# Latent attention by head: values stationary in two column halves, probabilities normalised before they are turned, gates produced turned, and changed places for sums and stops

## The chip, the cores and the metric

One core of one Trainium2 chip runs the whole program. The metric is the time of one execution in microseconds of device time (us). Below, TensorE, VectorE, ScalarE, GpSimd and SyncE are the core's engines; SyncE issues the loads of the weights.

## The reference, cut to what matters

Two blocks of two layers each work on x of 256 rows (tokens) and 1024 columns, all in float32. The first block mixes three attention branches. The second block has an even layer (windowed attention with a sink and a gated MLP, for x and for a context of 256 rows) and an odd layer with latent attention; the final norm follows.

```python
# even layer, for the 256 rows of x and the 256 rows of the context
q, k, v, u, vv, gate = split(h @ w_in0)
a = sink_attention(rope(q), rope(k), v)          # 8 heads of 64
b = gelu(u) * (w_s @ layer_norm(gelu(vv)) + b_s)
y = (concat(a, b) * silu(gate)) @ w_out0
# odd layer: latent attention, queries of x only, keys and values of x and context
q_a, kv_a, k_pe, gate = split(h @ w_in1)         # 256, 128, 32, 1024
q = rms_norm(q_a) @ w_qb                          # 16 heads of 64 + 32
k, v = rms_norm(kv_a) @ w_kvb                     # 16 heads, v of 64
p = softmax(q @ k.T * 96 ** -0.5)                 # 256 x 512 for each head
y = (concat_heads(p @ v) * silu(gate)) @ w_out1
# in every layer: shift, scale, gate = silu(c) @ w_ada + b_ada  (w_ada is 1024 x 3072)
```

## The kernel before, in words

Every engine's program is written out by hand, in order; nothing is rescheduled. Matmul results go to eight PSUM banks. A table of units (`units_of_layer_e`, `units_of_layer_o`) numbers every use of a bank, and `begin`, `done`, `filled`, `emptied` and `free` turn it into waits on two semaphores for each bank.

**The ring.** All weights are cut into chunks of up to 2 MB (`CH1`, `CHE`, `CHO`) that pass through three slots, in that order. SyncE has one program: it waits until the last user of chunk c-3 is done, and then issues the load of chunk c (L577). So a load also stands behind the waits of all loads before it. In the even layer the chunks are e_kv, e_q, e_u, e_vv, e_g0, adag4, e_ws, e_g1, adag5, ada0, ada1, e_o0, e_o1, ada2, ada3, and then those of the odd layer, o_kv, o_q, adah4, o_g0 and so on. An ada chunk is summed over its 1024 rows on TensorE in four column groups of 32 (`ada_rows`, L656), copied out by ScalarE, and brought to columns (`ada_columns`, L664).

**The start.** Four ada chunks are summed while x is normalised and turned; then the first projection, idx, waits for hT, which ScalarE and VectorE scale out of PSUM.

**Even layer.** `E_ORDER` is (2, 3, 0, 1): the context's row blocks first. The projections e_q, e_u and e_vv (`E_SPLIT`) are made of three fast products of high and low parts: ScalarE rounds rows to xhi and pieces of weights to whi, VectorE takes the differences xlo and wlo, TensorE multiplies (L1061). Then follow 15 steps g. In each TensorE does what the tables `E_GATES` (a gate projection of 8 matmuls of 512 columns, L1026), `E_SUMS` (`ada_rows`) and `E_ADA` (`ada_columns`) set for it, then turns two units of probabilities (L688, step 2 on), makes the logits of two units (L1115) and multiplies two turned units with the values (L1095, step 3 on). Step 4 has the gated MLP (L1146), steps 12 and 13 broadcast the gates gb (L1039). The output projection follows, with the remaining sums in `E_OUT_SUMS` and `E_OUT_ADA`.

**Odd layer.** o_kv, o_q, the gates o_g0 and o_g1 (rows on partitions), keys okT, values ova, queries oqT. The SiLU of all 2 x 1024 gate columns is one ScalarE operation (L1676). Then 16 steps of latent attention, two units (a block of 128 queries and a head) in each, by block first (`O_UNITS`). TensorE: logits of step p (L1243, 512 columns each), four transposes for each unit of step p-1 (L688), and four value matmuls for each unit of step p-2, with turned probabilities stationary and 64 columns of values moving (L1259). VectorE: maximum of each unit (L2478), its scaling (L2480), the copy of every second turned unit (L2484). ScalarE: exponentials (L1538) and the other copies (L1299). Per 8 heads `o_gated` scales by the reciprocal of the sums and multiplies with the gate (L2460, L2465). The result is turned with 16 transposes, copied to hT2, and projected.

## Time and profile before

| what | before |
|---|---|
| three runs, us | 1175.83, 1175.37, 1170.96; median 1175.37 |
| the profiled execution, us | 1175.9 (span 1174.1) |
| TensorE busy | 1118.2 us, 95% of the span |
| TensorE weight loads, beside it | 702.6 us, 60% |
| VectorE, ScalarE, GpSimd busy | 518.6 (44%), 410.6 (35%), 95.8 (8%) |
| chain that ended last | TensorE 82%, VectorE 8%, ScalarE 6%, DMA 3% |
| mean granted clock of TensorE | 0.988 |

The profiled execution is one run of the program; its span runs from the first instruction to the last, and its own time is 1.8 us longer. The chain is followed back from the last instruction, at each step to what released it. The even layer's steps stand at 771 to 895 us, its output projection at 896 to 964, the odd layer behind it, the latent attention at 1061 to 1137.

### The profile page before, as it was taken

To read this page: it belongs to the slowest core of one execution; us is meant where nothing else is said; L and a number is where in the kernel's file an instruction comes from. 1 tells how busy PE (TensorE), PEld (TensorE's weight loads), DVE (VectorE), ACT (ScalarE), POOL (GpSimd) and SP (SyncE) were. 2 spreads that over 40 slices of the span, in tenths; PEclk is the share of its full clock that TensorE was granted. 3 is DMA by queue.
4 is the path that set the end of the run, shared out by engine and by line. 5 is a ranking of instruction groups with operands and counts; after the bars stand their busy time and mean duration, and the time that the engine had idled before them with its cause. 6 is when DMAs were issued, how large, how long until landed. Compare 5 with 4: busy or idle time off the path is not lost.

```text
span 1174.1 us, 12609 instructions
## 1 busy us (share of the span) xinstructions
PE 1118.2 (95%) x4876; PEld 702.6 (60%) x4876; DVE 518.6 (44%) x1087; ACT 410.6 (35%) x858; POOL 95.8 (8%) x115
## 2 busy tenths in 40 slices
PE   5999999999999999999999989989999989999997
PEld 2687775644447878655444468845666437345773
DVE  2439765552425488542224342244424133235642
ACT  2436545320025355633300342253534032325431
POOL 3005110000000131100000003100000000230000
PEclk9899999999999999999999999999999998998999
DMA  9644333567334343245574251200415116241000
GB/s 376 232 181 172 149 144 115 214 245 286 143 113 173 157 183 144 104 151 213 210 286 179 78 212 72 90 1 9 208 63 224 72 30 253 80 157 76 1 1 36
DMA packets 13739, 171.23 MB, mean 146 GB/s; under 512 B 1504, under 2 KB 1760, under 8 KB 3056
## 3 DMA queue, kind: packets, MB, share of 16 engines
q1 hardware_dynamic: 12944, 167.77, 37.3%
q10 hardware_dynamic: 736, 2.65, 0.6%
q8 instruction: 39, 0.64, 0.2%
q14 instruction: 20, 0.16, 0.0%
HBM read 169.37 MB, written 1.05 MB: 145 GB/s over the span
## 4 chain that ended last, share of the span: by engine, by line
PE 82%; DVE 8%; ACT 6%; DMA 3%; issue 1%; ACTq 0%; DVEq 0%
PE bank L696 17%; PE bank L1026 16%; PE bank L718 11%; PE bank L990 7%; PE bank L1061 6%; PE bank L688 4%; PE bank L1243 3%; PE bank L1259 2%; PE bank L794 2%; DVE wlo L1986 2%; DMA ring<-in_weights 2%; PE bank L664 2%; PE bank L656 2%; DMA X<-in_x 1%; PE bank L1095 1%
## 5 line engine op out<-in xcount | busy, mean ns | idle before, releaser
L696 PE MATMUL bank<-ring,hT 128*128 128x512 f32 (+1 forms) x576 | 246.3, 584 | 3.2 <-ACT hT L1319 2.4
L1026 PE MATMUL bank<-ring,hT 128*128 128x512 f32 (+2 forms) x544 | 202.2, 530 | 10.1 <-DMA ring<-in_weights 6.3
L696 PEld LDWEIGHTS bank<-ring,hT 128*128 128x128 f32 x576 | 108.9, 193 | 123.3 <-issue 118.5
L1026 PEld LDWEIGHTS bank<-ring,hT 128*128 128x128 f32 x544 | 101.2, 196 | 102.3 <-issue 95.6
L1986 DVE TENSOR_TENSOR wlo<-ring,whi 128x512 fp32r<-128x512 f32 x120 | 89.0, 767 | 40.6 <-ACT whi L1375 40.4
L718 PE MATMUL bank<-whi,xhi 128*128 128x512 f32 (+1 forms) x256 | 99.1, 387 | 6.6 <-DVE wlo L1986 4.7
L718 PE MATMUL bank<-whi,xlo 128*128 128x512 f32 (+1 forms) x256 | 96.5, 377 | 0.0
L718 PE MATMUL bank<-wlo,xhi 128*128 128x512 f32 (+1 forms) x256 | 96.4, 377 | 0.0
L1375 ACT ACTIVATE whi<-ring 128x512 fp32r<-128x512 f32 x120 | 72.7, 630 | 64.3 <-PE bank L718 64.3
L718 PEld LDWEIGHTS bank<-whi,xhi 128*128 128x128 f32 x256 | 48.1, 188 | 21.5 <-issue 7.7
L1299 ACT ACTIVATE G<-bank 128x512 f32<-128x512 f32 x24 | 14.3, 596 | 119.7 <-PE bank L696 119.7
L990 PE MATMUL bank<-ring,X 128*128 128x512 f32 x128 | 55.9, 595 | 0.0
L718 PEld LDWEIGHTS bank<-whi,xlo 128*128 128x128 f32 x256 | 48.2, 188 | 9.1
L718 PEld LDWEIGHTS bank<-wlo,xhi 128*128 128x128 f32 x256 | 48.2, 188 | 7.9
L656 PE MATMUL bank<-ring,cst 128*32 128x512 f32 x224 | 31.5, 686 | 13.5 <-DMA ring<-in_weights 13.5
L1887 DVE SCALAR_TENSOR_TENSOR retqkv<-ring,cst,retqkv 128x512 f32<-128x512 f32 x56 | 42.1, 752 | 2.0
L990 PEld LDWEIGHTS bank<-ring,X 128*128 128x128 f32 x128 | 24.0, 190 | 28.7 <-issue 28.7
L1061 PE MATMUL bank<-whi,xhi 128*128 128x512 f32 x96 | 38.0, 396 | 2.7 <-issue 2.7
L1061 PE MATMUL bank<-wlo,xhi 128*128 128x512 f32 x96 | 38.4, 400 | 0.0
L1061 PE MATMUL bank<-whi,xlo 128*128 128x512 f32 x96 | 37.4, 389 | 0.0
L1299 ACT ACTIVATE LP<-bank 128x512 f32<-128x512 f32 x40 | 22.5, 595 | 39.3 <-PE bank L688 39.3
L2293 DVE TENSOR_TENSOR wlo<-ring,whi 128x1024 fp32r<-128x1024 f32 x12 | 15.4, 1292 | 44.5 <-ACT whi L1552 44.5
(380 smaller groups left out, 1558.5 us busy)
## 6 DMA issues: line engine op xcount, KB each, us to landing
ring<-in_weights SPq DMA_DIRECT2D x73, 2048.0 KB, 8.5
ring<-in_weights SPq DMA_DIRECT2D x5, 1024.0 KB, 5.1
ring<-in_weights SPq DMA_DIRECT2D x2, 1360.0 KB, 7.6
ring<-in_weights SPq DMA_DIRECT2D x1, 1536.0 KB, 9.5
kk<-in_k SPq DMA_DIRECT2D x1, 1120.0 KB, 8.0
X<-in_x ACTq DMA_DIRECT2D x1, 1024.0 KB, 15.8
kc<-in_k ACTq DMA_DIRECT2D x1, 1024.0 KB, 11.7
X<-in_context SPq DMA_DIRECT2D x1, 1024.0 KB, 10.7
```

The costliest lines, as they stand in the source:

```text
L656: mm = pe.matmul(ps[GROUP * g:GROUP * (g + 1), :], cst[:, k, :], ring[:, slot, k * 512:(k + 1) * 512], start=(k < 4), stop=(k >= 4))
L688: mm = pe.transpose(ps[0:n, i * P:(i + 1) * P], blk, ident[:])
L696: mm = pe.matmul(ps[:, 0:width], hT[:, k, t * P:(t + 1) * P], ring[:, slot, k * stride + w0:k * stride + w0 + width], start=(k == 0), stop ...
L718: mm = pe.matmul(o[:, 0:width], a, b[:, q % BUFFERS, at], start=(k == 0 and m == 0), stop=(k == KD - 1 and m == 2))
L990: mm = pe.matmul(ps[:, :], branchT[b][:, k, t * P:(t + 1) * P], ring[:, slot, k * D + h * 512:k * D + h * 512 + 512], start=(k == 0), stop ...
L1026: mm = pe.matmul(ps[:, 0:width], hT2[:, k, t * P:(t + 1) * P], ring[:, slot, k * width:(k + 1) * width], start=(k == 0), stop=(k == KD - 1))
L1061: mm = pe.matmul(o[:, :], a, b[:, q % 2, at], start=(k == 0 and n == 0), stop=(k == KD - 1 and n == 2))
L1243: done(u, f"ml{i}", pe.matmul(ps[:, :], oqT[:, h, t * P:(t + 1) * P], okT[:, h, :], start=True, stop=True))
L1299: act.activation(dst, shape_like(ps[0:dst.shape[0], 0:n], dst), func, scale=scale).then_inc(free(u, name), 1)
L1375: act.activation(whi1[:, q % BUFFERS, :], w, ACT.Copy).then_inc(event("hi1_ready"), 1)
L1887: ins = dve.scalar_tensor_tensor(rows, w, cst[:, k, v:v + 1], rows, ALU.mult, ALU.add)
L1986: dve.tensor_tensor(wlo1[:, q % BUFFERS, :], piece1(q)[2], whi1[:, q % BUFFERS, :], ALU.subtract).then_inc(event("lo1_ready"), 1)
```

## The change

- The latent attention goes by head: the two units of a step are the two query blocks of one head. VectorE normalises the probabilities (`o_normal`: reciprocal of the sum, scaling of 128x512 in place) before they are turned; it makes them in its step p+1, behind the maxima of that step. ScalarE copies all turned units to a new tile PT3. TensorE turns units two steps after their logits, ahead of the step's own logits, and every second step multiplies two heads (`o_values`): values stationary (64 columns), 256 query columns moving, one head in the lower and one in the upper half of the output partitions. The result is already turned: `o_gated` multiplies it with turned gates into hT2, and the 16 transposes and their copies are gone.
- The gates are produced turned (`gates_turned`): weights stationary, 256 row columns moving, 32 matmuls of 256 columns for each half in place of 16 of 512. SiLU of the first half is one ScalarE operation, that of the second half is done while its banks are copied. The scale of the logits moves to the copies of oqT, and the scaling of each maximum is gone.
- Chunk ada2 goes ahead of e_o0 and e_o1; the tables of the even layer's steps change: the second gate projection goes to step 1, adag4 is summed in step 2, adag5 in step 6 (was 9), ada0 in 9 (was 12), ada1 in 12 (was in the output projection).
- In the even layer the split products take row blocks in `E_ORDER`, wait for each block of xlo by itself, and ScalarE and VectorE round rows and weights in a new order.
- Nine matmuls of ones stand before the first projection of layer 0.
- The scratch size for DMA descriptors is 1024.

```diff
--- before.py
+++ after.py
        ("e_g0", KD * 512), ("adag4", KD * 512), ("e_ws", KD * P), ("e_g1", KD * 512), ("adag5", KD * 512),
-       ("ada0", KD * 512), ("ada1", KD * 512), ("e_o0", KD * 512), ("e_o1", KD * 512), ("ada2", KD * 512),
+       ("ada0", KD * 512), ("ada1", KD * 512), ("ada2", KD * 512), ("e_o0", KD * 512), ("e_o1", KD * 512),
        ("ada3", KD * 512)]
...
+BUSY_START = 9
...
-E_GATES = {0: 0, 2: 1, 3: 2, 5: 3, 7: 4, 8: 5, 10: 6, 11: 7}
-E_SUMS = {1: "adag4", 9: "adag5", 12: "ada0"}
-E_ADA = {2: "adag4", 10: "adag5", 13: "ada0"}
+E_GATES = {0: 0, 1: 1, 3: 2, 5: 3, 7: 4, 8: 5, 10: 6, 11: 7}
+E_SUMS = {2: "adag4", 6: "adag5", 9: "ada0", 12: "ada1"}
+E_ADA = {4: "adag4", 7: "adag5", 10: "ada0", 13: "ada1"}
 E_ROWS_AT = {12: 0, 13: 1}
-E_OUT_SUMS = {(0, 0): "ada1", (1, 0): "ada2", (1, 2): "ada3"}
-E_OUT_ADA = {(0, 2): "ada1", (1, 1): "ada2", (1, 3): "ada3"}
+E_OUT_SUMS = {(0, 1): "ada2", (1, 1): "ada3"}
+E_OUT_ADA = {(0, 3): "ada2", (1, 2): "ada3"}
...
-O_UNITS = [(t, h) for t in range(TT) for h in range(MLA_HEADS)]
+O_UNITS = [(t, h) for h in range(MLA_HEADS) for t in range(TT)]
...
-        og = sbo("og", [P, TT, D])
+        og = sbo("og", [P, KD, S])
+        PT3 = sbo("pt3", [P, 4, NT, TT, P])
...
+            def keep_busy(ps, n):
+
+                for i in range(n):
+                    pe.matmul(ps[:, 0:P], ones[:], ones[:], start=True, stop=True)
...
+                if l == 0:
+                    keep_busy(begin(u, "idx0"), BUSY_START)
...
-            pe.wait_ge(event("xlo_ready"), NT)
             for q in range(len(E_SPLIT) * SPLIT_PIECES):
                 name, i = E_SPLIT[q // SPLIT_PIECES], q % SPLIT_PIECES
                 pe.wait_ge(event("lo_ready"), q + 1)
-                for t in range(NT):
+                for n, t in enumerate(E_ORDER):
+                    if q == 0:
+                        pe.wait_ge(event("xlo_ready"), n + 1)
...
-            slot = landed2("o_g0")
-            for t in range(TT):
-                project2(u, f"o_g0{t}", slot, t, 512)
+            def gates_turned(n):
+
+                slot = landed2(f"o_g{n}")
+                for j in range(2):
+                    ps = begin(u, f"o_g{n}{j}")
+                    for a in range(2):
+                        for k in range(KD):
+                            at = k * 512 + (2 * j + a) * P
+                            mm = pe.matmul(ps[:, a * S:(a + 1) * S], ring[:, slot, at:at + P], hT2[:, k, 0:S],
+                                           start=(k == 0), stop=(k == KD - 1))
+                    done(u, f"o_g{n}{j}", mm)
+
+            gates_turned(0)
...
+            def o_turn(i):
+
+                pe.wait_ge(event("o_norm"), i + 1)
+                ps = begin(u, f"mp{i}")
+                done(u, f"mp{i}", turn_blocks(ps, [L2[:, i % 4, b * P:(b + 1) * P] for b in range(4)]))
+
+            def o_values(j):
+
+                for i in range(4 * j, 4 * j + 4):
+                    emptied(pe, u, f"mp{i}")
+                ps = begin(u, f"mo{j}")
+                for b in range(NT):
+                    for r in range(2):
+                        h = 2 * j + r
+                        mm = pe.matmul(ps[64 * r:64 * r + 64, 0:S].rearrange("p (t c) -> p t c", t=TT),
+                                       ova[:, b, h * 64:(h + 1) * 64], PT3[:, h % 4, b], start=(b == 0), stop=(b == NT - 1))
+                done(u, f"mo{j}", mm)
+
+            for p in range(MLA_HEADS + 3):
+                if 2 <= p < MLA_HEADS + 2:
+                    o_turn(2 * p - 4)
+                    o_turn(2 * p - 3)
...
-                if 1 <= p < 17:
-                    for i in (2 * p - 2, 2 * p - 1):
-                        emptied(pe, u, f"ml{i}")
-                        ps = begin(u, f"mp{i}")
-                        done(u, f"mp{i}", turn_blocks(ps, [L2[:, i % 4, b * P:(b + 1) * P] for b in range(4)]))
-                if p >= 2:
-                    for i in (2 * p - 4, 2 * p - 3):
-                        t, h = O_UNITS[i]
-                        emptied(pe, u, f"mp{i}")
-                        if i % 8 == 0:
-                            begin(u, f"mo{i // 8}")
-                        o = bank[u.at[f"mo{i // 8}"][0]]
-                        for b in range(NT):
-                            mm = pe.matmul(o[:, (h % 8) * 64:(h % 8) * 64 + 64], PT2[:, i % 4, b * P:(b + 1) * P],
-                                           ova[:, b, h * 64:(h + 1) * 64], start=(b == 0), stop=(b == NT - 1))
-                        if i % 8 == 7:
-                            done(u, f"mo{i // 8}", mm)
-            for t in range(TT):
-                pe.wait_ge(event("om_ready"), t + 1)
-                for h in range(2):
-                    ps = begin(u, f"oyT{t}{h}")
-                    done(u, f"oyT{t}{h}", turn_blocks(ps, [og[:, t, (4 * h + i) * P:(4 * h + i + 1) * P] for i in range(4)]))
+                if p >= 4 and p % 2 == 0:
+                    o_values(p // 2 - 2)
+            for j in range(MLA_HEADS // 2):
+                emptied(pe, u, f"mo{j}")
             slots = [landed2("o_o0"), landed2("o_o1")]
...
+            def rows_high(t):
+                emptied(act, u, f"xT{t}0")
+                emptied(act, u, f"xT{t}1")
+                act.activation(xhi[:, :, t * P:(t + 1) * P], hT2[:, :, t * P:(t + 1) * P], ACT.Copy).then_inc(event("xhi_ready"), 1)
+
             scale_x2(u, 0, E_ORDER[2])
             norm_x2(0, E_ORDER, E_PARTS, 1, "x_ready", X_E)
+            rows_high(E_ORDER[0])
+            rows_high(E_ORDER[1])
             scale_x2(u, 0, E_ORDER[3])
 
...
             split_high(0)
+            rows_high(E_ORDER[2])
+            rows_high(E_ORDER[3])
             split_high(1)
...
-            act.activation(og[:], og[:], ACT.Silu).then_inc(event("osilu"), 1)
+            act.activation(og[:, 0:4, :], og[:, 0:4, :], ACT.Silu).then_inc(event("osilu"), 1)
+            for j in range(2):
+                copy_out(u, f"o_g1{j}", og[:, 4 + 2 * j:6 + 2 * j, :], func=ACT.Silu)
...
+                copy_rows(u, f"oqT{j}", oqT[:, 2 * j:2 * j + 2, :], ps[0:MLA_QK, :].rearrange("p (a b) -> p a b", a=2),
+                          ACT.Copy, scale=MLA_SCALE)
+            for p in range(MLA_HEADS + 2):
+                if p >= 2:
+                    for i in (2 * p - 4, 2 * p - 3):
+                        t, h = O_UNITS[i]
+                        copy_out(u, f"mp{i}", PT3[:, h % 4, :, t])
...
+            rows_low(0)
+            rows_low(1)
+            split_low(0)
+            rows_low(2)
+            rows_low(3)
+            for q in range(1, len(E_SPLIT) * SPLIT_PIECES):
+                split_low(q)
...
+            def o_gated(j):
+
+                dve.wait_ge(event("osilu"), 1)
+                for i in range(2):
+                    emptied(dve, u, f"o_g1{i}")
+                ps = filled(dve, u, f"mo{j}")
+                dve.tensor_tensor(hT2[:, j, 0:S], ps[:, 0:S], og[:, j, :], ALU.mult).then_inc(free(u, f"mo{j}"), 1)
+
+            def o_normal(i):
+
+                t, h = O_UNITS[i]
+                emptied(dve, u, f"ml{i}")
+                step(dve.reciprocal(r2[:, t, h:h + 1], sm2[:, t, h:h + 1]))
                 settle()
+                dve.tensor_scalar(L2[:, i % 4, :], L2[:, i % 4, :], r2[:, t, h:h + 1], None, ALU.mult).then_inc(event("o_norm"), 1)
+
+            for p in range(MLA_HEADS + 4):
+                if p < MLA_HEADS:
+                        dve.tensor_reduce(mx2[:, t, h:h + 1], ps[:, :], AX, ALU.max, negate=True).then_inc(event("o_max"), 1)
+                if 1 <= p < MLA_HEADS + 1:
+                    o_normal(2 * p - 2)
+                    o_normal(2 * p - 1)
+                if p >= 5 and p % 2:
+                    o_gated((p - 5) // 2)
+    nc = _bacc.Bacc("TRN2", target_bir_lowering=False, num_devices=1, dynamic_dma_scratch_size=1024)
```

TensorE in the even layer, from the gate projection of step 5 to that of step 7. Before:

```order
L1026 MATMUL bank<-ring,hT 128x512 x8
L688 MATMUL bank<-ident,LP 128x128 x8
L1115 MATMUL bank<-ekT,eqT 128x512 x2
L1095 MATMUL bank<-ev,LP 128x64 x8
L688 MATMUL bank<-ident,LP 128x128 x8
L1115 MATMUL bank<-ekT,eqT 128x512 x2
L1095 MATMUL bank<-ev,LP 128x64 x8
L1026 MATMUL bank<-ring,hT 128x512 x8
```

The same place in the change (its lines stand higher by 8 or 9):

```order
L1034 MATMUL bank<-ring,hT 128x512 x8
L694 MATMUL bank<-ident,LP 128x128 x8
L1124 MATMUL bank<-ekT,eqT 128x512 x2
L1104 MATMUL bank<-ev,LP 128x64 x8
L657 MATMUL bank<-ring,cst 32x512 x8
L694 MATMUL bank<-ident,LP 128x128 x8
L1124 MATMUL bank<-ekT,eqT 128x512 x2
L1104 MATMUL bank<-ev,LP 128x64 x8
L1034 MATMUL bank<-ring,hT 128x512 x8
L665 MATMUL bank<-col,ert 128x16 x4
```

The sum of adag5 (L657) now stands one step behind the gate projection, and its columns (L665) in the step after.

TensorE in the latent attention, two steps in the middle. Before:

```order
L1243 MATMUL bank<-okT,oqT 128x512 x2
L688 MATMUL bank<-ident,LP 128x128 x8
L1259 MATMUL bank<-ova,LP 128x64 x8
L1243 MATMUL bank<-okT,oqT 128x512 x2
L688 MATMUL bank<-ident,LP 128x128 x8
L1259 MATMUL bank<-ova,LP 128x64 x8
```

In the change:

```order
L694 MATMUL bank<-ident,LP 128x128 x8
L1281 MATMUL bank<-okT,oqT 128x512 x2
L694 MATMUL bank<-ident,LP 128x128 x8
L1281 MATMUL bank<-okT,oqT 128x512 x2
L1269 MATMUL bank<-pt,ova 64x256 x8
```

The turns stand ahead of the logits, and the values come once in two steps.

VectorE there, one step. Before:

```order
L2478 TENSOR_REDUCE mx<-bank 128x1
L2480 TENSOR_SCALAR mx<-mx 128x1
L2478 TENSOR_REDUCE mx<-bank 128x1
L2480 TENSOR_SCALAR mx<-mx 128x1
L2484 COPY LP<-bank 128x512
```

In the change:

```order
L2507 TENSOR_REDUCE mx<-bank 128x1 x2
L2498 RECIPROCAL r<-sm 128x1
L2500 TENSOR_SCALAR LP<-LP,r 128x512
L2498 RECIPROCAL r<-sm 128x1
L2500 TENSOR_SCALAR LP<-LP,r 128x512
```

The copy and the scalings of the maxima have gone, and the normalisation of the step before stands behind the two maxima.

## Rows read from the trace of the kernel before

**Rows 1.** The page, busy time of TensorE (us, share, instructions).

```profile
PE 1118.2 (95%) x4876; PEld 702.6 (60%) x4876; DVE 518.6 (44%) x1087; ACT 410.6 (35%) x858; POOL 95.8 (8%) x115
```

**Rows 2.** Waits of TensorE, 700 to 1174: total, times, longest (us).

```profile
PE bank L1026 <- DMA ring<-in_weights: 6.3, 3, 4.9
PE bank L1061 <- issue: 2.7, 1, 2.7
...
PE bank L1115 <- DVE LP L2344: 1.7, 1, 1.7
```

**Rows 3.** Windows: length, busy PE PEld DVE ACT POOL, PEclk, DMA share, GB/s.

```profile
36.40:43.20 6.80, 5.75 (x11) 3.75 (x12) 5.57 (x12) 6.29 (x13) 0.00 (x0) 0.50 1.01 430
766.80:773.60 6.80, 5.41 (x32) 3.88 (x31) 1.19 (x4) 6.39 (x17) 0.00 (x0) 1.00 0.00 0
886.30:889.70 3.40, 3.40 (x8) 1.86 (x8) 2.45 (x5) 1.34 (x2) 0.00 (x0) 0.50 0.97 414
968.20:975.00 6.80, 5.75 (x22) 5.78 (x23) 0.95 (x2) 0.30 (x1) 0.00 (x0) 0.50 1.01 420
1060.40:1067.20 6.80, 6.12 (x9) 2.56 (x9) 3.14 (x7) 3.32 (x6) 0.00 (x0) 0.50 0.23 92
```

**Rows 4.** The chain, even layer, 819 to 865: start, us, what.

```profile
820.06 8.21 DMA ring<-in_weights
...
835.44 0.87 PE bank L688 x8
...
839.30 6.92 PE bank L1026 x16
...
862.88 0.80 PE bank L664 x8
```

**Rows 5.** Transfers issued from 819 to 834: KB each, us to landing.

```profile
ring<-in_weights SPq DMA_DIRECT2D x3, 2048.0 KB, 13.0
```

**Rows 6.** The chain where the odd layer begins.

```profile
964.39 4.62 DMA ring<-in_weights
...
969.25 7.43 PE bank L1026 x32
...
979.14 4.60 PE bank L1026 x32
```

**Rows 7.** Timeline of VectorE there: start, us, engine, line.

```profile
967.74 1.42 DVE L1954 TENSOR_SCALAR Y<-X,st 128x1024 f32<-128x1024 f32 x2
```

**Rows 8.** Groups by form: busy us, mean ns, idle before (TensorE, its loads, VectorE).

```profile
L656 PE MATMUL bank<-ring,cst 128*32 128x512 f32 x224 | 31.5, 686 | 13.5 <-DMA ring<-in_weights 13.5
...
L1026 PE MATMUL bank<-ring,hT 128*128 128x256 f32 x96 | 21.3, 380 | 1.6 <-ACT hT L1342 1.6
...
L1201 PEld LDWEIGHTS bank<-X,ring 128*64 128x64 f32 x32 | 4.3, 137 | 9.4 <-issue 8.8 <-ACT X L1538 0.6
...
L2478 DVE TENSOR_REDUCE mx<-bank 128x1 f32<-128x512 f32 x32 | 22.1, 691 | 26.1 <-PE bank L1243 26.1
...
L2301 DVE TENSOR_SCALAR evv<-evv,st 128x512 f32<-128x512 f32 x4 | 2.0, 488 | 0.1
...
L1911 DVE RECIPROCAL st<-st 128x1 f32<-128x1 f32 x4 | 0.7, 163 | 2.2 <-ACT st L1312 2.2
```

**Rows 9.** Timeline of TensorE after the last gate products.

```profile
1054.02 2.78 PE L688 MATMUL bank<-ident,Y 128*96 128x128 f32 x24
...
1058.65 1.08 PE L688 MATMUL bank<-ident,Y 128*96 128x128 f32 x8 [1.85 <-ACT oqT L1538]
```

**Rows 10.** The chain in and after the latent attention.

```profile
1077.54 1.73 PE bank L1259 x16
1079.27 1.77 PE bank L1243 x4
...
1129.23 0.88 PE bank L688 x8
...
1138.91 27.55 PE bank L1026 x64
```

More of the change, by code:

```diff
@@ L280, in units_of_layer_o @@
     u += [(f"oqT{j}", turn()) for j in range(8)] + [("adah5", proj())]
-    for p in range(16 + 2):
-        if p < 16:
+    for p in range(MLA_HEADS + 3):
+        if 2 <= p < MLA_HEADS + 2:
+            u += [(f"mp{2 * p - 4}", 6), (f"mp{2 * p - 3}", 7)]
+        if p < MLA_HEADS:
             b = (4, 0)[p % 2]
@@ L286, in units_of_layer_o @@
             u += [(f"gb0{h}", proj()) for h in range(2)]
-        if 1 <= p < 17:
-            u += [(f"mp{2 * p - 2}", 6), (f"mp{2 * p - 1}", 7)]
-        if p >= 2:
-            i = 2 * p - 4
-            if i % 8 == 0:
-                u.append((f"mo{i // 8}", 2 + (i // 8) % 2))
-    u += [(f"oyT{t}{h}", turn()) for t in range(TT) for h in range(2)]
+        if p >= 4 and p % 2 == 0:
+            u.append((f"mo{p // 2 - 2}", 2 + (p // 2) % 2))
     u += [(f"oout{t}{h}", turn()) for t in range(TT) for h in range(2)]
@@ L534, in piece_used @@
             if q % SPLIT_PIECES == SPLIT_PIECES - 1:
-                filled(eng, le, f"{E_SPLIT[q // SPLIT_PIECES]}{NT - 1}")
+                filled(eng, le, f"{E_SPLIT[q // SPLIT_PIECES]}{E_ORDER[-1]}")
             else:
@@ L1220, in _ @@
                     done(u, f"oqb{t}{c}", mm)
[L1221 to L1223 removed]
+            gates_turned(1)
             pe.wait_ge(event("oq_rot"), 1)
@@ L1237, in _ @@
             pe.wait_ge(event("okT_ready"), 1)
-            for p in range(16 + 2):
-                if p < 16:
+            def o_turn(i):
[12 more added lines that the diff above has]
+                done(u, f"mo{j}", mm)
+            for p in range(MLA_HEADS + 3):
+                if 2 <= p < MLA_HEADS + 2:
+                    o_turn(2 * p - 4)
+                    o_turn(2 * p - 3)
+                if p < MLA_HEADS:
                     for i in (2 * p, 2 * p + 1):
@@ L1653, in _ @@
             act.activation(st2[:, 48:54], st2[:, 40:46], ACT.Sqrt).then_inc(event("o_std2"), 1)
-            for t in range(TT):
-                copy_out(u, f"o_g0{t}", og[:, t, 0:512])
+            for j in range(2):
+                copy_out(u, f"o_g0{j}", og[:, 2 * j:2 * j + 2, :])
             ps = filled(act, u, "kvT")
@@ L1693, in _ @@
                         copy_out(u, f"gb0{h}", gbr[:, 0, h * 512:(h + 1) * 512])
-            for t in range(TT):
-                copy_out(u, f"oyT{t}0", hT2[:, 0:4, t * P:(t + 1) * P])
             for t in range(TT):
@@ L2284, in _, with rows_low, split_low @@
             scale_x2(u, 0, E_ORDER[3])
-            for i, t in enumerate(E_ORDER):
+            def rows_low(i):
                 dve.wait_ge(event("xhi_ready"), i + 1)
-                c = slice(t * P, (t + 1) * P)
+                c = slice(E_ORDER[i] * P, (E_ORDER[i] + 1) * P)
                 dve.tensor_tensor(xlo[:, :, c], hT2[:, :, c], xhi[:, :, c], ALU.subtract).then_inc(event("xlo_ready"), 1)
-            for q in range(len(E_SPLIT) * SPLIT_PIECES):
+            def split_low(q):
                 w = piece(q)[2]
@@ L2477, in _ @@
                         ps = filled(dve, u, f"ml{i}")
-                        step(dve.tensor_reduce(mx2[:, t, h:h + 1], ps[:, :], AX, ALU.max, negate=True))
-                        settle()
-                        dve.tensor_scalar(mx2[:, t, h:h + 1], mx2[:, t, h:h + 1], MLA_SCALE, None, ALU.mult).then_inc(event("o_max"), 1)
-                if 1 <= p < 17:
-                    i = 2 * p - 1
-                    ps = filled(dve, u, f"mp{i}")
-                    dve.tensor_copy(PT2[:, i % 4, :], ps[:, :]).then_inc(free(u, f"mp{i}"), 1)
-                if p >= 6 and (p - 6) % 4 == 0:
-                    o_gated((p - 6) // 4)
-            for t in range(TT):
-                ps = filled(dve, u, f"oyT{t}1")
-                dve.tensor_copy(hT2[:, 4:8, t * P:(t + 1) * P], ps[:, :].rearrange("p (k c) -> p k c", k=4)).then_inc(free(u, f"oyT{t}1"), 1)
+                        dve.tensor_reduce(mx2[:, t, h:h + 1], ps[:, :], AX, ALU.max, negate=True).then_inc(event("o_max"), 1)
[4 more added lines that the diff above has]
+                    o_gated((p - 5) // 2)
             for t in range(TT):
```

50 lines of the change are left out of this document (7 added, 43 removed).

## The prediction, made before the changed kernel ran

> **What bounds the kernel now.** I read the page's busy shares, then TensorE's waits in the second half, then the chain and the transfers around the places that the diff touches, then the windows for the clock, and last the groups by form for prices. TensorE is busy 95% of the span [rows 1]. It waits little, so a gain has to come from fewer or cheaper matmul passes, from one of the few waits [rows 2], or from stretches in which the granted clock was 0.50, which is the lower level, 1.2 of 2.4 GHz [rows 3]. The kernel is a list of passes: a loss on TensorE's own path counts whole, and so does a gain. In the trace each float32 matmul is two passes. All sums are made against the profiled execution: 1175.9 us for a span of 1174.1, 0.5 above the median of the runs (1175.37).
>
> **The change part by part** (minus is a gain).
>
> *a. Warm-up matmuls before the first projection.* TensorE sits idle before that projection and then works 5.75 us at 0.50 in the window from 36.4 [rows 3]. Nine 128-column matmuls are 18 passes, about 0.11 each by the transposes (0.87 for 8) [rows 4], so 2.0 us, placed where TensorE waits for hT anyway: their own cost is nothing; if that wait were gone it would be 2.0. If they hold the clock, 5.75 busy us at half speed shrink by 2.9. I take -2.9; the bounds are 0 and -2.9.
>
> *b. Split rows pipelined in the even layer.* TensorE waits 2.7 us once before the split products, for all four row blocks of xlo [rows 2]. The change asks only for the first block and moves two roundings on ScalarE ahead. Each block feeds 6 matmuls, and xlo of the next one is made meanwhile. -2.7; bounds 0 and -2.7.
>
> *c. Blocks in the order 2, 3, 0, 1 there.* ScalarE still empties e_vv in the order 0 to 3, and block 0 is now third. It starts two blocks late, catches up in part, and its copies of eqT, on which the first gate projection waits, end about 1.7 us later. Behind it the wait of 1.7 for VectorE's LP [rows 2] goes, because 6.9 us of gate projection now stand in front of it, and some of the wait for eu in step 4 too. Net -0.8; bounds -2 and +2.
>
> *d. adag5 summed in step 6, not 9.* This is the largest term. SyncE issues loads in ring order, and e_g1 (the next chunk) waits for the end of the gate projection of step 5. adag5 stands behind it in the queue. In the trace that moment is 820.04: e_g1 is there 8.2 us later [rows 4], and of the three loads issued together the middle one, adag5, lands 13.0 after its issue [rows 5], some 13.2 after the projection. Before, TensorE had two steps of turns, logits and values (3.86 each, 835.44 to 839.30) [rows 4] and then needed e_g1: the wait was short. Now it has one step, 3.9, and then needs adag5: it idles 9.3 us. Behind such an idle the clock is low, as after the DMA wait at 964, where 5.75 busy us ran at 0.50 [rows 3]: +2.9. The short wait at step 7 goes, -0.6. Sum +11.6; bounds +8.7 (clock holds) and +12.2. The sum and its columns are moved, not added.
>
> *e. ada1 summed in step 12, not in the output projection.* Its load waits for the last gate projection, in step 11, and is needed 3.9 us later; it takes 8.2, like e_g1: idle 4.3, then 2.9 for the low clock. In exchange a short wait for gbr's copy (about 1) is covered and the low stretch at 886, 3.40 busy us at 0.50 [rows 3], which cost 1.7, is replaced. +4.5; bounds +1.6 and +7.2.
>
> *f. ada2 ahead of e_o0 and e_o1.* o_kv's load waited for the last product of e_o1, so TensorE waited 4.62 us and then ran at 0.50: both passes of o_kv took 7.43, against 4.60 for the same work later [rows 6]. Now o_kv waits for e_o0, long done. From 964.37 to the end of the fourth o_kv product were 19.4 us (983.74) [rows 6]. Now: 4.6; then the normalised rows, finished 4.8 after 964.37 (VectorE at 967.74, 1.42 long) [rows 7]; the turns and their scaling 2.5 (976.68 to 979.14); 4.6 more: 12.0. o_g0's load hangs on that end before and after, so the gain arrives whole: -7.4. Bounds -7.4 and -4.6.
>
> *g. Gates turned.* 32 passes of 512 columns become 64 of 256 for each half. A 256-column pass takes 0.222 (21.3/96) [rows 8], so 14.2 against 13.8: +0.8 for both. The smaller scratch size for DMA descriptors touches none of the queues used here: nothing.
>
> *h. SiLU of the gates.* The last oqT turns waited 1.85 us for ScalarE, which did one SiLU over both halves after the last gate product [rows 9]. Now half is done earlier and the other half rides on the copy. 32 transposes (3.5) and the ada columns (0.80) [rows 4] then stand alone between the last gate product and the logits: 4.4 instead of 7.2 (1054.02 to 1061.22). -2.8. And the logits began at 0.50, 6.12 busy us of it in the window from 1060.4 [rows 3]; with the shorter gap I take the clock to hold. About 1 of those 3 us comes back, since exponentials and gbr copies then hold the second pair: -2.0; bounds 0 and -3.
>
> *i. The latent attention.* Before, each of the 16 steps was logits 1.77, turns 0.88, values 1.73 (1077.54 to 1079.27) [rows 4, 10], 4.38 us. The values are now 8 matmuls of 256 columns per two steps. If the two column halves run side by side, that is 8 x 0.222 plus a little, 1.9 per two steps: TensorE alone would need 3.6 a step. But the normalisation now stands between. The turns of step p need o_norm, and VectorE makes it behind the maxima of step p-1, the second of which waits for the logits just before those turns. From the end of those logits: maximum 0.69, twice (reciprocal 0.16, settle 0.04, scaling of 128x512 0.49) [rows 8], handovers 0.05 each: 2.15; then the second turn 0.44 and the logits 1.77: 4.37. So a step without values takes 4.4, not 2.65; one with values 1.9 + 0.88 + 1.77 = 4.55. Fourteen steps from the end of the second logits pair: 8 x 4.37 + 6 x 4.55 = 62.3, against 59.6 (one of 2.6, thirteen of 4.38): +2.7. The saved value time is lost to the new wait. ScalarE takes over VectorE's copy of the turned blocks, one more in each step; it is idle for most of this stage, so that is hidden; without that cover it would be one copy a step. Bounds: -1 if VectorE's operations overlap more, and +13.7 below.
>
> *j. The end.* Before, 9.7 us from the last logits (1129.23) to the projection (1138.91) [rows 10]: turns, value groups, scaling and gating, 16 transposes and a copy. Now: 2.6 + 1.9 + 0.9 + a copy 0.65 + 1.9 + gating 0.5 = 8.5: -1.2.
>
> Sum: -2.9 - 2.7 - 0.8 + 11.6 + 4.5 - 7.4 + 0.8 - 4.8 + 2.7 - 1.2 = -0.2. Forecast 1176 us: no change that counts. A measurement of this kernel can tell about 0.5% (5.9 us) from nothing.
>
> **Rule against row, once for the halves.** Four column groups of 32 share the array in the trace: 224 passes of 512 columns took 31.5 us, 0.14 each, where one alone takes 0.43 (6.92 for 16) [rows 4, 8]. Their weight loads are hidden too. The Trainium skill, "TensorE: Matmul & The Clock Gate", Part 3, says that a weight load overlaps running matmuls only when the row group differs. Here both halves use all rows; by that rule 16 loads of 64 columns (0.137 each [rows 8]) would stand outside the products of every head pair, 2.2 us x 8, some 17 us more. The trace speaks against it for 32-wide groups; no row shows it for 64.
>
> **Rule against row, for the clock.** Between 766.80 and 773.60 transposes and an idle stretch ran and the clock stayed 1.00; around 1054 to 1061 it fell after more of both [rows 3]. The same page, Part 4, says that transposes do not count as work for the clock. By it h would keep its low stretch, 2.0 us more.
>
> **The rivals.**
> 1. *The halves do not run side by side, or their loads don't hide* (slower). Values then cost 3.5 per pair: six steps of 6.1 and two groups at the end: +10.2 + 3.4 = +13.6, so 1189; with the loads outside 1193. It decides from 2.3 us per pair upward, where values plus turns pass the 2.6 of VectorE's chain. Against it: the four 32-wide groups [rows 8]. Chance 0.11.
> 2. *The clock gains don't come* (slower): the warm-up is too little (+2.9), the logits start slow (+2.0), and the longer gap of c, now 3 us, makes the gates start slow (+1.7). 1182.6. For it: all these gaps stay partly filled with small passes. Chance 0.17.
> 3. *Idle stretches in d and e are cheaper* (faster): the clock is back at once after both (-5.8) and VectorE's chain is a little shorter (-1): 1169 or below. For it: the clock's timing differs from run to run. The idle itself cannot shrink, as the queue's order is fixed. Chance 0.24.
> 4. *The warm-up does nothing* but the rest holds: 1178.6, inside my forecast's own case.
>
> **How the numbers follow.** My forecast's case has 0.48. Rival 3 gives faster by over 0.5%: 0.24. Rivals 1 and 2 give slower: 0.28. The range must leave out no more than 2 in 10: it reaches from 1165, below rival 3, to 1188, which takes in rival 2 and the edge of rival 1.
>
> **What would show it.** Right: in the even layer a TensorE wait of 9 us for the ring before an ada sum, another of 4 after the last gate; no wait at the start of the odd layer; TensorE waiting for VectorE's scaled LP in every latent step without values, steps of 4.4; value groups of 1.9. Wrong: value groups of 3.5 (rival 1); latent steps near 3.6, which would mean that VectorE's chain is no bound, and 10 us less; no ring wait in step 6, which would mean that I misread the queue, and 11 less; clock at 0.50 around 36 or 1060 (rival 2).

## The result, and the profile after

The changed kernel took 1177.61 us (median of 11 runs, 1171.77 to 1179.54), the kernel before 1174.32 (11 runs, 1166.11 to 1175.83). The ratio is 1.004, 95% interval 1.0022 to 1.0059: slower by less than the half per cent that I called no change. The forecast was 1176.0. The profiled execution took 1177.28 for a span of 1175.5.

The page, busy time, answers to [rows 1]. TensorE is busy 14.5 us less and the span is 1.4 longer: what the side-by-side values, the 16 dropped transposes and less work at the slow clock save is idled away.

```profile
PE 1103.7 (94%) x4814; PEld 689.0 (59%) x4814; DVE 516.3 (44%) x1097; ACT 420.3 (36%) x872; POOL 96.6 (8%) x115
```

Where it idles: the waits of TensorE from 700 on (total, times, longest), against [rows 2].

```profile
PE bank L657 <- DMA ring<-in_weights: 14.1, 2, 9.7
PE bank L694 <- DVE LP L2500: 12.4, 9, 1.4
PE bank L1034 <- ACT eqT L1317: 2.5, 1, 2.5
```

The 2.7 us before the split products and most of the 6.3 for the ring at the old places are gone. Two new kinds of wait stand there: for the loads of adag5 and ada1 (9.7 and 4.4 us), and for VectorE's scaling in the latent attention.

The chain in the even layer (start, us, what) shows the first of them. The transfer issued after the last product of step 5 lands 13.1 later, as in [rows 5]; TensorE has turns, logits and values for some 3.5 us of that.

```profile
805.41 6.94 PE bank L1034 x16
...
812.75 13.10 DMA ring<-in_weights
...
825.88 3.64 PE bank L657 x16
...
874.59 6.94 PE bank L1034 x16
881.54 8.16 DMA ring<-in_weights
...
889.75 3.69 PE bank L657 x16
```

Both sums take 3.64 and 3.69 where the same 16 passes take 1.85 at the full clock. Windows (length, busy time of TensorE, its granted clock, DMA share, GB/s), against [rows 3]:

```profile
36.40:43.20 6.80, 6.80 (x35) 1.00 0.99 417
...
818.30:831.90 13.60, 6.01 (x26) 0.50 0.77 329
886.50:893.40 6.90, 3.65 (x17) 0.51 0.99 423
900.20:903.60 3.40, 3.40 (x7) 0.50 0.78 333
968.20:975.10 6.90, 6.90 (x21) 1.00 0.00 0
1060.40:1067.20 6.80, 5.20 (x16) 1.00 0.60 253
```

The low stretches at 36, 968 and 1060 are gone; the one at 818 is new, and around 886 there is more than before. The chain where the odd layer begins, against [rows 6]: no DMA between the last e_o product and the first o_kv product, which now form one run of 48 passes.

```profile
965.96 1.75 PE bank L694 x16
967.71 11.22 PE bank L1034 x48
...
981.45 4.60 PE bank L1034 x32
...
986.06 8.44 DMA ring<-in_weights
...
994.54 14.10 PE bank L1204 x64
```

And the chain in two steps of the latent attention, against [rows 10]:

```profile
1103.82 0.69 DVE mx L2507
1104.52 0.08 DVE r L2498
1104.62 0.50 DVE LP L2500
1105.16 1.25 PE bank L694 x8
1106.41 1.72 PE bank L1281 x4
1108.13 1.88 PE bank L1269 x16
1110.01 1.02 PE bank L694 x8
1111.04 1.73 PE bank L1281 x4
```

A step without values runs through VectorE (a maximum, a reciprocal, a scaling); a step with values needs 1.88 + 1.02 + 1.73 = 4.63 and waits for nobody.

### The profile page after: what moved, and what is told of

Same layout as the page of the kernel before. It is cut to its first block, busy times and chain, and to the rows that moved or that the text cites. A ratio compares the mean times of both kernels' runs of the same rounds, so it can differ in the third digit from the quotient of the medians.

```text
span 1175.5 us, 12529 instructions
## 1 busy us (share of the span) xinstructions
PE 1103.7 (94%) x4814; PEld 689.0 (59%) x4814; DVE 516.3 (44%) x1097; ACT 420.3 (36%) x872; POOL 96.6 (8%) x115
## 3 DMA queue, kind: packets, MB, share of 16 engines
q10 hardware_dynamic: 736, 2.65, 0.6%
## 4 chain that ended last, share of the span: by engine, by line
PE 82%; DVE 7%; ACT 5%; DMA 4%; issue 1%; ACTq 0%; SPq 0%; DVEq 0%
PE bank L702 17%; PE bank L1034 14%; PE bank L724 11%; PE bank L998 7%; PE bank L1070 6%; PE bank L694 5%; DMA ring<-in_weights 3%; PE bank L1204 2%; PE bank L802 2%; PE bank L1281 2%; PE bank L657 2%; DVE wlo L2009 2%; PE bank L665 2%; DMA X<-in_x 1%; PE bank L1104 1%; PE bank L1269 1%
## 5 line engine op out<-in xcount | busy, mean ns | idle before, releaser
L702 PE MATMUL bank<-ring,hT 128*128 128x512 f32 (+1 forms) x576 | 243.5, 578 | 1.1 <-ACT retqkv L1317 0.6
L702 PEld LDWEIGHTS bank<-ring,hT 128*128 128x128 f32 x576 | 107.3, 190 | 120.1 <-issue 114.1
L1034 PE MATMUL bank<-ring,hT 128*128 128x512 f32 (+2 forms) x480 | 170.9, 513 | 5.9 <-ACT eqT L1317 2.5
L1034 PEld LDWEIGHTS bank<-ring,hT 128*128 128x128 f32 x480 | 86.4, 190 | 82.5 <-issue 77.4
L657 PE MATMUL bank<-ring,cst 128*32 128x512 f32 x224 | 33.8, 730 | 27.5 <-DMA ring<-in_weights 27.5
L694 PE MATMUL bank<-ident,LP 128*128 128x128 f32 x224 | 32.8, 287 | 12.4 <-DVE LP L2500 12.4
L694 PEld LDWEIGHTS bank<-ident,LP 128*128 128x128 f32 x224 | 25.7, 146 | 31.2 <-DVE LP L2500 21.4
```

The source lines that it names most:

```text
L657: mm = pe.matmul(ps[GROUP * g:GROUP * (g + 1), :], cst[:, k, :], ring[:, slot, k * 512:(k + 1) * 512], start=(k < 4), stop=(k >= 4))
L694: mm = pe.transpose(ps[0:n, i * P:(i + 1) * P], blk, ident[:])
L702: mm = pe.matmul(ps[:, 0:width], hT[:, k, t * P:(t + 1) * P], ring[:, slot, k * stride + w0:k * stride + w0 + width], start=(k == 0), stop ...
L1034: mm = pe.matmul(ps[:, 0:width], hT2[:, k, t * P:(t + 1) * P], ring[:, slot, k * width:(k + 1) * width], start=(k == 0), stop=(k == KD - 1))
```

## The experiments

Base is the changed kernel (1177.61, ratio 1.004) unless said. The kernel before ran beside each set of experiments, 8 to 20 times, with medians of 1173.1 to 1173.7. The times given are medians of 4 to 12 runs, the ratios are against the kernel before, with their 95% interval. Each experiment has one profile; "the path" compares the start of the same instruction in two profiles.

### 1. The even layer's sums at their old places (terms d and e)

```diff
-E_SUMS = {2: "adag4", 6: "adag5", 9: "ada0", 12: "ada1"}
...
-E_OUT_SUMS = {(0, 1): "ada2", (1, 1): "ada3"}
+E_SUMS = {2: "adag4", 9: "adag5", 12: "ada0"}
...
+E_OUT_SUMS = {(0, 0): "ada1", (1, 0): "ada2", (1, 2): "ada3"}
```

The columns (E_ADA, E_OUT_ADA) moved with them, and the loads run ada1, e_o0, ada2, e_o1, ada3.

> The changed kernel with the even layer's sums back in steps 9 and 12 and in the output projection, and ada2 between e_o0 and e_o1, so that o_kv's load still waits only for e_o0. Theory (terms d and e: TensorE idles for the ring because adag5 and ada1 are asked for too early): the two idle stretches of 9.6 and 4.4 us and most of the slow clock behind them go, about 15 us of the 15.9 that the trace shows for d and e, so 1162 to 1164, and the first o_kv product still starts right behind the last e_o product. Rival (the ring is the bound in this layer: its loads land as fast as they can, and TensorE waits for one of them wherever the sums stand): the wait comes back at e_o0, ada2 or e_o1, and the time stays above 1170.

Measured: 1162.3, ratio 0.9902 (0.9867 to 0.9938). The chain of this kernel at the same places:

```profile
807.99 6.94 PE bank L1034 x16
814.95 8.68 DMA ring<-in_weights
...
823.67 7.13 PE bank L1034 x16
...
873.75 1.90 PE bank L657 x16
```

The transfer is still in the chain, but two steps now stand beside it, and TensorE's only ring wait from 800 to 975 is 1.0 us:

```profile
PE bank L1034 <- DMA ring<-in_weights: 1.0, 1, 1.0
```

Against the changed kernel this one is 2.6 us later after the first gate projection (1.2 from ahead of it, the rest because its clock was low at 767) and 13.3 earlier at the last e_o product: 15.9 gained between. The rival falls: the ring is not the bound of this layer, the place of the sums made it one.

### 2. Scaling ahead of the maxima (term i)

```diff
             for p in range(MLA_HEADS + 4):
+                if 1 <= p < MLA_HEADS + 1:
+                    o_normal(2 * p - 2)
+                    o_normal(2 * p - 1)
                 if p < MLA_HEADS:
...
-                if 1 <= p < MLA_HEADS + 1:
-                    o_normal(2 * p - 2)
-                    o_normal(2 * p - 1)
```

> The changed kernel with VectorE's order turned in the latent attention: in each step first the scaling of the previous pair, then the maxima of the pair just computed. Nothing is left out. Theory (term i: the turns wait because the scaling stands behind the next pair's maxima): a step without values goes from 4.34 us towards 2.9 (two maxima 1.4, one exponential 0.65, one scaling 0.66, handovers), one with values stays at 4.5, the mean step is some 3.7 instead of 4.49, so 9 to 12 us less: 1166 to 1169. Rival (ScalarE's two exponentials and two copies are the bound, or the wait is only handed on to the exponentials): steps stay at or over 4.2, and less than 4 us is gained.

Measured: 1158.72, ratio 0.9873 (0.9821 to 0.9926). The gain is larger than the 9 to 12 us that I expected: 18.9 in the medians, 16.1 between the two profiled spans. The chain of this kernel, from the logits of a long step on:

```profile
1100.20 1.72 PE bank L1281 x4
1101.92 0.88 PE bank L694 x8
1102.79 1.72 PE bank L1281 x4
1104.51 1.88 PE bank L1269 x16
```

The wait for LP is gone from the list, not shortened: steps are 2.60 and 4.62, mean 3.61. My 2.9 for the short step forgot that what ScalarE and VectorE need for a pair has to fit only the mean step (VectorE's own work for a pair is some 2.9 us, an estimate from 0.69 for a maximum, 0.15 and 0.49 for reciprocal and scaling, each twice, and the gating): a long step gives them the time that the next short one lacks. Eight short steps make 8 x 1.74 = 13.9; the tail after the last logits is 1.7 shorter as well.

### 3. The two heads one after the other (rival 1)

```diff
-                for b in range(NT):
-                    for r in range(2):
+                for r in range(2):
+                    for b in range(NT):
```

> The changed kernel with the two heads of a value group one after the other instead of in turn, so that no two passes of different column halves stand next to each other. Nothing is left out. Theory (the halves share the array side by side, as 1.88 us for 16 passes says against 3.55 for 16 x 0.222): value groups take 3.5 us, steps with values 6.1 to 6.3, and the time is 12 to 14 us more, about 1190. Rival (a pass of 64 output columns is simply cheaper, whatever stands beside it): groups stay at 1.9 and the time at 1177.

Measured: 1183.93, ratio 1.0087 (1.0057 to 1.0117), 6.3 above the changed kernel: neither number. The chain shows groups of 2.79 instead of 1.88:

```profile
1096.85 1.72 PE bank L1281 x4
1098.57 2.79 PE bank L1269 x16
```

The starts in the records explain the size. In the changed kernel the passes of one half are 0.216 apart, and those of the other half start 0.006 behind each: 8 x 0.216 = 1.7 for 16 passes. In this kernel passes of one half are also 0.216 apart, but the second half's passes begin 0.92 us into the group, beside the fifth pass of the first half: four passes of each half run as pairs, four of each alone, and 12 x 0.216 = 2.6. So a pass alone is not cheaper and a neighbour is what helps: the mechanism of the theory holds, and its price of 3.5 (12 to 14 us more in all) missed by taking no overlap at the seam. Over the eight groups 0.91 each make 7.3; the profiled spans differ by 4.8.

### 4. Term f alone, on the kernel before

```diff
-       ("ada0", KD * 512), ("ada1", KD * 512), ("e_o0", KD * 512), ("e_o1", KD * 512), ("ada2", KD * 512),
+       ("ada0", KD * 512), ("ada1", KD * 512), ("e_o0", KD * 512), ("ada2", KD * 512), ("e_o1", KD * 512),
```

> The kernel before with one edit: ada2 stands ahead of e_o1 in the order of the loads, so that the load of o_kv waits for e_o0 and no longer for the last product of e_o1. Theory (term f): the wait of 4.6 us at the start of the odd layer and the slow clock behind it go, the rest of the program is the same, and the gain arrives whole: 7.4 us less, 1167. Rival (o_g0's load is then the late one and takes the gain back): the first o_g0 product starts less than 4 us earlier.

Measured: 1163.1, ratio 0.991 (0.9882 to 0.9938). The chain:

```profile
954.99 11.31 PE bank L1026 x48
...
973.43 8.50 DMA ring<-in_weights
```

TensorE is 2.4 us earlier than in the kernel before at the last e_o product (ahead of the wait), 10.3 earlier at the end of the fourth o_kv product and 10.3 at the first o_g0 product: 7.9 for the term, where 7.4 was expected, and it arrives whole. The profiled span is 12.3 shorter. The other 4 us are not the edit's: this profile has no low stretch at 886 and none at 1060, in code that did not change. That shows how much of a single profile's clock is the run's. The medians are 10.4 apart, so part of those 4 us shows in the four runs of this kernel as well.

### 5. Work in the idle stretches (the clock's share of d and e)

```diff
+                    keep_busy(begin(u, "s_" + E_SUMS[g]), {6: 42, 12: 18}.get(g, 0))
                     ada_rows(u, E_SUMS[g], landed2(E_SUMS[g]))
```

> The changed kernel with 42 and 18 matmuls of 128 x 128 (two passes of 0.11 each) placed in steps 6 and 12 just ahead of the wait for adag5 and for ada1: 9.2 and 4.0 us of work that nobody uses, in the time in which TensorE waits for the ring. Nothing is left out. Theory (the second part of terms d and e: the low clock behind the two stretches comes from the idling itself): the granted clock stays at 1.00 from 815 to 905, and 4 to 5 us are gained, about 1173. Rival (the low clock has another cause, or the fillers delay the sums by what they save): a low stretch remains, or the time stays within 1.5 us of 1177.

Measured: 1173.99, ratio 1.0011 (0.9994 to 1.0028), 3.6 below the changed kernel, whose interval (1.0022 to 1.0059) it still touches. The chain:

```profile
818.23 9.43 PE bank L688 x84
827.66 1.85 PE bank L657 x16
```

and two windows of it (columns as above):

```profile
818.30:831.90 13.60, 13.60 (x115) 1.00 0.93 396
886.50:893.40 6.90, 6.74 (x49) 1.00 1.00 430
```

The theory holds: with TensorE at work through the same waits the granted clock stays at 1.00 (2.4 GHz) and adag5's sum is back at 1.85, ada1's at 1.97. From the first logits to the o_g0 products 7.0 us are gained on the changed kernel; this run stood 2.0 behind it at the first logits, most of it from a low stretch at 765.

### 6. Without the warm-up (term a)

```diff
-                if l == 0:
-                    keep_busy(begin(u, "idx0"), BUSY_START)
```

> The changed kernel without the nine warm-up matmuls ahead of the first projection. Theory (term a: they keep the granted clock at 1.00 through the wait for hT): a stretch at 0.50 is back near 36, TensorE's work in it takes 2.5 to 3 us more, and the even layer starts 2.9 later than in the changed kernel; about 1180. Rival (the clock there differs from run to run, and the better start of the changed kernel was chance): no stretch at 0.50 near 36 and no difference.

Measured: 1179.34, ratio 1.0051 (1.0031 to 1.0071); the intervals of the two kernels overlap, so the times alone do not separate them. The window does:

```profile
34.20:41.10 6.90, 5.63 (x11) 0.51 1.01 433
```

A stretch at 0.50 near 36 is in all three profiles without the warm-up (before, experiments 4 and 6) and in none of the ten with it. At the second projection this kernel is 2.4 us later, 2.8 net of a prologue that was 0.4 earlier, against the 2.9 of the theory. The first logits came 4.0 later, 1.7 of it from a low stretch at 768.

### 7. One late SiLU (term h)

```diff
-            act.activation(og[:, 0:4, :], og[:, 0:4, :], ACT.Silu).then_inc(event("osilu"), 1)
...
-                copy_out(u, f"o_g1{j}", og[:, 4 + 2 * j:6 + 2 * j, :], func=ACT.Silu)
+                copy_out(u, f"o_g1{j}", og[:, 4 + 2 * j:6 + 2 * j, :])
...
+            act.activation(og[:], og[:], ACT.Silu).then_inc(event("osilu"), 1)
```

> The changed kernel with one SiLU over both halves of the odd layer's gates after the last copy, as in the kernel before, instead of one half early and the other on the copy. Theory (term h: that long operation on ScalarE holds the last transposes, and the longer gap lets the clock fall): a wait of 1.5 to 2 us for ScalarE's oqT copies, a stretch at 0.50 at the first logits, 3 to 5 us more: 1181 to 1182. Rival (the gain of h is the wait alone and the clock holds in any case): 1.5 to 2 us more, no low stretch.

Measured: 1181.07, ratio 1.0056 (1.0034 to 1.0078). TensorE's timeline there, to be held against [rows 9], and the window at the first logits:

```profile
1055.89 2.78 PE L694 MATMUL bank<-ident,Y 128*96 128x128 f32 x24
1060.52 1.08 PE L694 MATMUL bank<-ident,Y 128*96 128x128 f32 x8 [1.85 <-ACT oqT L1556]
```

```profile
1060.40:1067.20 6.80, 5.55 (x24) 1.00 0.51 212
```

The wait is back to the hundredth, worth 1.9 us on the path, and in this profile the clock holds, as the rival has it. The times do not bear the rival out: the median is 3.5 above the changed kernel's, the ratio 0.16% (1.9 us), and the ten runs fall into four of 1174.9 to 1178.6 (mean granted clock 0.987 to 0.991), the profiled one among them, and six of 1180.2 to 1184.3 (0.980 to 0.987), where the slowest of the changed kernel took 1179.54. Where those six lose their time no profile shows. Nor do the profiles settle it: three have the long gap ahead of the first logits, the kernel before (0.50 there), experiment 4 and this one (1.00); the ten with the short gap are all at 1.00. The wait is shown; whether the late SiLU also costs clock stays open.

### 8. ScalarE in TensorE's order (term c)

```diff
-            for t in range(NT):
+            for t in E_ORDER:
                 ps = filled(act, u, f"e_vv{t}")
```

and the same for e_q and e_u.

> The changed kernel with ScalarE emptying e_q, e_u and e_vv in the order 2, 3, 0, 1, in which TensorE now ends them. Theory (term c: ScalarE starts e_vv two blocks late, since it waits for block 0): the wait for eqT ahead of the first gate projection goes from 2.5 back to 1.4, the projection starts 1.1 earlier, and the stretch at 0.50 of 3.4 us that most profiles with the changed order show there (767) goes too, which is another 1.7. In total 1 to 3 us less than the changed kernel, 1175 to 1176.5; part of it may be lost again in the wait for adag5, whose load does not depend on it. Rival (the order on ScalarE does not matter, ekT and eqT are the chain): the wait for eqT stays at 2.5.

Measured: 1175.98, ratio 1.0032 (1.0013 to 1.005), 1.6 less than the changed kernel but not to be told from it by the times. The waits tell it:

```profile
PE bank L1034 <- ACT eqT L1317: 1.4, 1, 1.4
```

The projection starts 1.16 us sooner after the split products, as the theory had it (1.1). The low stretch behind this gap depends on its length as far as the profiles go: with a wait of 2.5, 7 of 9 have one near 767 (those of the changed kernel and of experiment 9 do not), with 1.4 none of 4.

### 9. All rows at once (term b)

```diff
-                        pe.wait_ge(event("xlo_ready"), n + 1)
+                        pe.wait_ge(event("xlo_ready"), NT)
```

with the four row blocks made ahead of the first piece on both engines.

> The changed kernel with the split rows as before: ScalarE and VectorE make all four blocks of the high and low rows ahead of the first piece of weights, and TensorE waits for all four. Theory (term b): the wait of 2.7 us ahead of the split products is back and nothing else changes, so the first gate projection starts 2.5 to 3 us later and the time is about 1180. Rival (the pieces of the weights are the later ones there, so that the order of the rows gains nothing): under 1 us.

Measured: 1179.64, ratio 1.0066 (1.0041 to 1.0092). In the chain the rows stand alone ahead of the products again:

```profile
690.27 4.63 DVE xlo L2310 x4
```

The split products start 2.9 us later than in the changed kernel, net of 0.9 that came from the prologue. "Nothing else changes" did not hold: this profile has a stretch at 0.50 from 697 to 701, right behind the wait, that makes the products 1.5 longer, and the first gate projection starts 4.4 later net. The medians are 2.0 apart and the two intervals overlap, so the times alone do not separate these kernels.

### 10. Both repairs, and all three

Experiments 1 and 2 together:

> Both edits together: sums back in steps 9 and 12 with ada2 between e_o0 and e_o1, and VectorE's scaling ahead of the maxima. If the two costs lie in different layers and are independent, the gains add: 1151 to 1155, below both kernels by over 1.5%. Rival (an earlier end of the even layer makes the odd layer's loads late, o_q or o_g0 first): 5 us or more of it comes back as a ring wait in the odd layer.

Measured: 1146.37, ratio 0.9758 (0.9718 to 0.9797): some 5 us below the range that I gave, since the second edit alone had given more than expected. No ring wait in the odd layer is longer than 0.4 us, so the rival falls. With ScalarE's order of experiment 8 too:

> The two edits that lowered the time (sums in steps 9 and 12 with ada2 between e_o0 and e_o1; VectorE's scaling ahead of the maxima) and ScalarE's copies of e_q, e_u and e_vv in the order 2, 3, 0, 1. If the wait for eqT shrinks by 1.1 here as in the kernel with that edit alone and the clock holds behind it, and no ring wait takes it back (there is none left in these steps), this gives 1 to 3 us under the 1146.4 of the two edits: 1143.5 to 1145.5, below both kernels. Rival (a load becomes the bound again): no gain over 1146.4.

Measured: 1142.53, ratio 0.9748 (0.9721 to 0.9776), 1.0 below the range given; the two intervals overlap, so the third edit's part stands on its wait alone. This kernel's waits from 700 on:

```profile
PE bank L1034 <- ACT eqT L1317: 1.4, 1, 1.4
PE bank L665 <- ACT gbr L1317: 1.0, 1, 1.0
PE bank L1034 <- DVE hT L2492: 1.0, 1, 1.0
```

No ring wait over 1 us and none for LP. By the spans the two edits gain 13.4 and 16.1 apart and 31.6 together, by the medians 15.3 and 18.9 apart and 31.2 together: additive within 3 us, so the two costs were independent of each other. With the three repairs the change makes the kernel 2.5% faster than before.

## Why the prediction was right, step by step

The time came out, and most steps with it, but part of the hit is luck. Below, "early" and "late" compare the same instruction in the profiles of the kernel before and of the changed one. The sum was -0.2 and the spans differ by +1.4. The sum was too low by 2.1 in d and e, by 0.9 in h and in j, by 0.5 in c and 0.2 in i; against that stand 0.8 in f, 0.6 in g and 0.4 in b, and 1.6 us at the start of the run that are not the change's at all; the last 0.4 is rounding and what follows the start of the last projection.

- **Warm-up (a), -2.9.** Measured -2.9: TensorE is 1.6 us early at the last ada columns of the prologue (the run's, not the change's: the first record of its clock at 1.00 stands at 26.4 instead of 29.6) and 4.4 early at the second projection. Experiment 6 confirms the mechanism.
- **Split rows (b), -2.7.** From 4.4 early before them to 7.5 early at the first split product: -3.1; experiment 9 puts 2.9 on it.
- **Order (c), -0.8.** The wait for eqT grew by 1.1, and 1.4 came back by step 5: -0.3. Rival 2's low clock at 767 was no rare case but the usual one; the profiled run lacked it.
- **Sums (d and e), +16.1.** The right mechanism, read from the queue's order alone, and experiment 1 gives 15.9. In the profile itself they cost 18.2: from 7.7 early at the end of step 5 to 13.2 late after the values, less 2.65 for ada1's passes, which came from the output projection. The idle stretches were 9.7 and 4.4 against 9.3 and 4.3; the rest is mostly in e (6.2 against 4.5): two low stretches where I had one in the place of another, and the wait of 1.0 for gbr's copy, which I had taken as covered and which is still there.
- **ada2's place (f), -7.4.** 13.2 late to 2.3 late is 10.9, less the same 2.65: -8.2; experiment 4 says 7.9.
- **Gates turned (g), +0.8.** 14.08 against 14.00 in the first half and 13.98 against 13.90 in the second: +0.2. I had priced the old form at 13.8 and the new one at 14.2. Right in sign, too small to matter. That the smaller scratch size costs nothing was not tested.
- **SiLU (h), -2.8 and -2.0.** From the last gate product to the first logits 7.0 became 5.1: -1.9, not -2.8, since 0.8 of issue time stands ahead of the logits that my 4.4 left out. From there to the end of the second pair of logits 8.5 became 6.5: -2.0, as forecast. The weak step is the reason given for it, "with the shorter gap I take the clock to hold". It did hold, but in the profiles of experiments 4 and 7 it held with the longer gap too. The sum was made against one profile's clock, which I took for the kernel's; whether the gap decides stays open.
- **Latent attention (i), +2.7.** Measured +2.9, with steps of 4.34 and 4.63 for 4.37 and 4.55. That the new wait takes what the values save is shown by experiment 2.
- **The end (j), -1.2.** The projection starts 1.2 late and the last logits ended 1.5 late: -0.3. What I mis-sized is the handover: the last values stand behind two copies of ScalarE, 1.09 in the chain where I had one of 0.65, and I had priced none of the issue time (0.24 and 0.45) around them.

**Rule against row, the halves.** 128 loads of 64 columns and 128 passes (mean 385 ns each) fit into eight groups of 1.9; the loads stand outside nowhere. The groups by form in the changed kernel:

```profile
L1269 PE MATMUL bank<-pt,ova 128*64 128x256 f32 x128 | 15.6, 385 | 0.9 <-ACT pt L1317 0.9
L1269 PEld LDWEIGHTS bank<-pt,ova 128*64 128x64 f32 x128 | 8.7, 136 | 9.2 <-issue 4.7 <-ACT pt L1317 1.1
```

So rival 1 fell; its own sum was somewhat high, too (3.5 instead of 1.9 for eight groups is 12.8, not 13.6). The Trainium skill, "TensorE: Matmul & The Clock Gate", Part 3, says in one sentence that a load overlaps running matmuls only when the row group differs, and in another that a load into the background weight buffer is pulled ahead as well. Both halves use all rows here: the trace disagrees with the first sentence and leaves room for the second.

**Rule against row, the clock.** The changed kernel's chain between the gates and the logits:

```profile
1056.65 3.49 PE bank L694 x32
1060.14 0.80 PE bank L665 x8
```

3.49 us of transposes left the clock at 1.00 behind them, in experiments 4 and 7 also with 1.85 us of idling in their midst; in the profile of the kernel before, with the same idling, the clock was 0.50 behind them [rows 3]. The Trainium skill, "TensorE: Matmul & The Clock Gate", Part 4, does not count transposes as work for the clock. The prediction's reading of it, that h would keep its low stretch, did not come true in any of the ten profiles with the short gap. One low stretch in three profiles with the long gap neither supports nor refutes the rule.

## What to carry to other kernels

When work that consumes a streamed weight is moved earlier, ask for its load what frees its slot and how much other work then stands beside the transfer; here that arithmetic gave 16 us of loss before a run, and putting the sums back where they had been (adag5 three steps later) removed it. When an operation is put between two stages of a pipeline, put it on its engine ahead of what waits for newer data: the same instructions in another order took 16 us off. And a stretch of low clock in one profile is not a property of the kernel until other profiles show it; look at its idle gap and at a second run before pricing it.

## What the runs showed that I had not expected

- Two matmuls of different column halves run together even when not ordered for it: at the seam of two serial heads four passes of each half still ran as pairs (2.79 us instead of 16 x 0.216 = 3.5). By the starts, the second head's first pass ran at 0.920 us, ahead of the first head's sixth at 1.130, which stands earlier in the program.
- The same code is at 0.50 in one profile and at 1.00 in another: the first latent logits in one of the two profiles of that code (before and experiment 4), and a stretch between 16 and 29 us in 10 of 13. In the other three (before, changed, experiment 2) the trace has no record of the clock ahead of 26 us. The profile's windows print 1.00 there, yet the 16 passes of the first ada sum take 3.64 us, not the 1.9 of a full clock: where no record stands, go by the passes.
- Filling a wait with useless matmuls paid: 13.4 us of them, where nothing else could run, gained 7.0 us on the path and 3.6 in the medians, because the useful work behind ran at 2.4 instead of 1.2 GHz.
